# Top-k routing of 16 experts: places of the chosen tokens from a scan, indices sorted later, the gate applied at the addition

## The chip, the cores and the metric

One core of a Trainium2 chip runs the whole program in one launch. The metric is the device time of one execution in microseconds, the median of several runs. The core's engines are TensorE (PE in the profile; its weight loads are the row PEld), VectorE (DVE), ScalarE (ACT) and GpSimd (POOL). SyncE (SP) issues nearly all transfers from device memory.

## The reference

Two blocks one after the other on 256 tokens of width 1024, all float32. The change lies in the first block's expert layer:

```python
def _expert_choice_ffn(xn, router_w, w_gate, w_up, w_down):
    cap = EC_CAPACITY * T // N_EXPERTS                       # 2 * 256 / 16 = 32
    probs = softmax(einsum('btd,de->bte', xn, router_w))     # 256 tokens, 16 experts
    gate, idx = lax.top_k(swapaxes(probs, 1, 2), cap)        # each expert chooses 32 tokens
    xg = xn[bidx, idx]
    h = silu(einsum('becd,edf->becf', xg, w_gate)) * einsum('becd,edf->becf', xg, w_up)
    y = einsum('becf,efd->becd', h, w_down) * gate[..., None]
    return zeros_like(xn).at[bidx, idx].add(y)
```

Each expert's three matrices are 1024x2048, 1024x2048 and 2048x1024 in float32, 8 MB each, 24 MB an expert. The order of an expert's 32 tokens is free as long as gather, gate and scatter agree on it.

## The kernel before

The kernel is written engine by engine, each with its own list of instructions; semaphores (`S.name`, `wait_ge`) tie them together, so the order on an engine is the order in the code. `link(...)` on VectorE makes the next instruction wait until this one has ended.

The first mixer ends with the output product (`mix1_pe`, `mix1_dve`), which adds to the residual `hres` (128 tokens by two tiles by 1024). Then the routing: `route_transposes` and `route_rows` bring the normalised rows into channel order, 32 matmuls (line 836) give the logits, ScalarE and VectorE the softmax `probs` (lines 886 to 906: tokens in partitions, 16 experts wide). TensorE transposes it into `probT`: 16 partitions, 256 tokens wide.

On `probT` VectorE runs four rounds (lines 910 to 914), each finding the next 8 of the 32 largest (`max`), their indices (`max_index`) and overwriting them by -1 (`match_replace`). The indices as floats `topf` are spread into a block-diagonal `spread` of 16x512, which one matmul with ones broadcasts to all 128 partitions (line 847, `bank[4]`): in each partition the 512 token indices of 16 experts by 32 places. Two more matmuls (line 851) put the indices and the gates as columns into `bank[5]`. VectorE compares the broadcast with the token number of each partition (line 926): this gives `sel`, for each token tile a 0/1 matrix of tokens by (expert, place), first for the first pair of experts, then for the rest. `gather` (line 869) multiplies the normalised token rows with `sel`: 16 matmuls for a pair of experts, and `take_xg` (line 937) scales the result into `xg`, the input of the pair.

While VectorE searches, TensorE has nothing of use to do, and `keep_busy` (line 824) issues filler matmuls of 512 columns, whose result nobody reads: one in front of the transpose of the probabilities and six behind it.

The experts run in pairs (`expert_pair`). A piece of weights is 2 MB; an expert has 12 (4 gate, 4 up, 4 down), and 16 matmuls use a piece (lines 969 and 985). The pieces go through a ring of 8 slots; `slot_used` counts the pieces done, and SyncE (`experts_sync`, `load_slot`, line 1060) waits for it before it overwrites a slot. The very first piece lies in `early`, so nine pieces can be loaded before the first expert begins. Of each expert the chain is gate and up products, silu on ScalarE, product on VectorE (`hgu`, line 1035), transposes, down product, ScalarE's copy to `yo` times the gate (line 1018), and the scatter: a matmul with `selT` (line 997), which VectorE builds per expert by comparing `iota` with the column of indices `idx_now` (line 1032), and four additions to `hres` (line 1043). The first pair's code is written out (its index is the integer 0); the middle ones are a loop.

Behind the experts comes the second block, which neither the change nor its data touch.

## Time and profile before

| | |
|---|---|
| median of 3 runs | 1481.41 us (1478.77 to 1485.8) |
| the profiled execution | 1486.1 us, its span 1484.3 us, mean granted clock 0.874 |
| busy | PE 1103.4 (74%), PEld 630.8, VectorE 366.8 (25%), ScalarE 302.4, GpSimd 301.4 |
| the chain that ended last | DMA 56%, PE 37%, VectorE 5%, ScalarE 1% |
| memory | 475.88 MB read, 321 GB/s over the span |
| experts' weights | 191 transfers of 2048 KB into the ring, 35.7 to 36.0 us each from issue to landing |

In the rows below, times are us from the span's start. A row of the timeline gives start, duration, engine, line and operation, what it writes and reads, how many it merges, and in brackets the idle time before it with who ended it. In a row by stretch, each engine has its busy time and count; then come the clock granted to TensorE (1.00 is 2.4 GHz, 0.50 is 1.2 GHz), the busy share of the transfer engines and the bytes they moved. A float32 matmul appears as two passes.

### The profile page before, as it was taken

To read this page: it belongs to the slowest core of one execution; us is meant where nothing else is said; L and a number is where in the kernel's file an instruction comes from. 1 tells how busy PE (TensorE), PEld (TensorE's weight loads), DVE (VectorE), ACT (ScalarE), POOL (GpSimd) and SP (SyncE) were. 2 spreads that over 40 slices of the span, in tenths; PEclk is the share of its full clock that TensorE was granted. 3 is DMA by queue.
4 is the path that set the end of the run, shared out by engine and by line. 5 is a ranking of instruction groups with operands and counts; after the bars stand their busy time and mean duration, and the time that the engine had idled before them with its cause. 6 is when DMAs were issued, how large, how long until landed. Compare 5 with 4: busy or idle time off the path is not lost.

```text
span 1484.3 us, 19442 instructions
## 1 busy us (share of the span) xinstructions
PE 1103.4 (74%) x8303; PEld 630.8 (42%) x8303; DVE 366.8 (25%) x698; ACT 302.4 (20%) x435; POOL 301.4 (20%) x153
## 2 busy tenths in 40 slices
PE   6999986665766666656666665565668699899997
PEld 6998631211311211211211211121127688899996
DVE  5486510100100000001001000010026834653343
ACT  5753210000000000000000000000025335543431
POOL 5895000000000000000000000000015544376560
PEclk9999988968878878888887888888889799899999
DMA  9510989999999999999999999999997323466540
GB/s 283 171 33 23 425 329 429 426 428 428 428 428 429 429 427 429 429 427 429 429 427 430 428 427 429 429 427 428 428 393 180 98 91 109 158 200 196 170 143 29
DMA packets 94711, 478.04 MB, mean 322 GB/s; under 512 B 11035, under 2 KB 64154, under 8 KB 70074
## 3 DMA queue, kind: packets, MB, share of 16 engines
q1 hardware_dynamic: 94064, 476.28, 79.8%
q8 instruction: 48, 0.79, 0.2%
q10 hardware_dynamic: 585, 0.86, 0.2%
q14 instruction: 14, 0.11, 0.0%
HBM read 475.88 MB, written 1.25 MB: 321 GB/s over the span
## 4 chain that ended last, share of the span: by engine, by line
DMA 56%; PE 37%; DVE 5%; ACT 1%; issue 1%; SPq 0%; DVEq 0%; ACTq 0%
DMA ring<-in_expert_w_down 20%; DMA ring<-in_expert_w_gate 19%; PE bank L1238 19%; DMA ring<-in_expert_w_up 17%; PE bank L1975 4%; PE bank L969 4%; PE bank L985 1%; PE bank L409 1%; PE bank L426 1%; DVE work L1753 1%; DVE slot_r L1213 1%; PE bank L422 1%; PE bank L824 0%; PE bank L1389 0%; DVE work L1762 0%
## 5 line engine op out<-in xcount | busy, mean ns | idle before, releaser
L969 PE MATMUL bank<-ring,work 128*32 128x512 f32 x2032 | 315.8, 755 | 212.0 <-DMA ring<-in_expert_w_up 125.1
L969 PEld LDWEIGHTS bank<-ring,work 128*32 128x32 f32 x2032 | 61.9, 124 | 458.3 <-DMA ring<-in_expert_w_up 207.2
L1213 POOL TENSOR_TENSOR slot_r<-ring,slot_r 128x1024 fp32r<-128x1024 f32 (+1 forms) x60 | 217.9, 3646 | 136.1 <-ACT slot_r L1190 136.1
L985 PE MATMUL bank<-ring,work 128*32 128x512 f32 x1024 | 157.2, 748 | 91.4 <-DMA ring<-in_expert_w_down 88.0
L1221 POOL TENSOR_TENSOR slot_r<-ring,slot_r 128x512 fp32r<-128x512 f32 x16 | 21.5, 1363 | 975.8 <-ACT slot_r L1190 964.7
L1238 PE MATMUL bank<-slot_r 128*128 128x256 f32 (+1 forms) x1056 | 163.5, 296 | 10.3 <-DVE chan L2258 4.7
L1238 PEld LDWEIGHTS bank<-slot_r 128*128 128x128 f32 x1056 | 148.5, 202 | 14.7 <-DVE chan L2258 4.9
L1035 DVE TENSOR_TENSOR work<-work,bank 128x512 f32<-128x512 f32 x16 | 11.0, 687 | 511.5 <-PE bank L969 511.5
L1238 PE MATMUL bank<-work_r,slot_r 128*128 128x256 f32 x704 | 128.2, 283 | 1.2 <-DVE chan_r L1709 1.2
L1190 ACT ACTIVATE slot_r<-ring 128x2048 fp32r<-128x2048 f32 x63 | 118.3, 1903 | 1.8 <-DMA ring<-in_w_in 1.8
L1043 DVE TENSOR_TENSOR hres<-hres,bank 128x512 f32<-128x512 f32 x64 | 44.0, 687 | 299.3 <-PE bank L997 299.3
L985 PEld LDWEIGHTS bank<-ring,work 128*32 128x32 f32 x1024 | 31.7, 124 | 199.3 <-DMA ring<-in_expert_w_down 132.7
L1238 PEld LDWEIGHTS bank<-work_r,slot_r 128*128 128x128 f32 x704 | 110.3, 191 | 1.9 <-issue 1.5
L1238 PE MATMUL bank<-chan_r,slot_r 128*128 128x256 f32 x352 | 99.4, 283 | 0.0
L997 PE MATMUL bank<-chan,work 128*128 128x512 f32 x128 | 67.4, 665 | 13.2 <-ACT chan L1018 13.2
L1213 DVE TENSOR_TENSOR slot_r<-ring,slot_r 128x1024 fp32r<-128x1024 f32 x42 | 67.2, 1602 | 32.6 <-ACT slot_r L1190 32.5
L1018 ACT ACTIVATE chan<-bank,work 128x512 f32<-128x512 f32 x32 | 20.2, 683 | 266.6 <-PE bank L985 266.6
L1012 ACT ACTIVATE work<-bank 128x512 f32<-128x512 f32 x16 | 9.6, 597 | 313.9 <-PE bank L975 313.9
L1238 PEld LDWEIGHTS bank<-chan_r,slot_r 128*128 128x128 f32 x352 | 67.0, 190 | 0.4
L1010 ACT ACTIVATE work<-bank 128x512 f32<-128x512 f32 x16 | 9.6, 597 | 275.9 <-PE bank L969 275.9
L1975 PE MATMUL bank<-slot_r,work_r 128*128 128x512 f32 x264 | 63.1, 395 | 0.0
L1975 PEld LDWEIGHTS bank<-slot_r,work_r 128*128 128x128 f32 x264 | 48.9, 188 | 11.0
(388 smaller groups left out, 1025.8 us busy)
## 6 DMA issues: line engine op xcount, KB each, us to landing
ring<-in_expert_w_up SPq DMA_DIRECT2D x64, 2048.0 KB, 36.0
ring<-in_expert_w_down SPq DMA_DIRECT2D x64, 2048.0 KB, 35.8
ring<-in_expert_w_gate SPq DMA_DIRECT2D x63, 2048.0 KB, 35.7
ring<-in_w_in SPq DMA_DIRECT2D x23, 1024.0 KB, 8.1
ring<-in_w_ffn_gate SPq DMA_DIRECT2D x11, 1024.0 KB, 5.5
ring<-in_w_ffn_up SPq DMA_DIRECT2D x11, 1024.0 KB, 5.3
ring<-in_w_ffn_down SPq DMA_DIRECT2D x11, 1024.0 KB, 5.0
ring<-in_w_out SPq DMA_DIRECT2D x8, 1024.0 KB, 5.1
```

What stands on the lines that cost most here:

```text
L409: ins = pe.matmul(bank[2 * i][a, cs(h)], level_tile(i)[a, cs(h)], eye[a] if li == 0 else xm(i)[a, cs(h)], start=True, stop=True)
L422: ins = pe.matmul(wing(bank[2 * i + 1], 0)[a, cs(h)], xtm(i)[a, cs(h)], p1m(i)[a, cs(h)], start=True, stop=True)
L969: ins = pe.matmul(bank[b][32 * j:32 * j + 32, :], xg[:, 2 * s + kk, a * CAP:(a + 1) * CAP], w_[:, kk * FF + j * W5:kk * FF + (j + 1) * W5] ...
L985: ins = pe.matmul(bank[YB[dh]][32 * q:32 * q + 32, :], hT[:, q * P + 32 * s:q * P + 32 * s + 32], w_[:, q * D + dh * W5:q * D + (dh + 1) * ...
L997: pe.matmul(bank[(LAST_SB[t] if final else SB)[dh]][:, :], selT[:, t * P:(t + 1) * P], yo[:, dh * W5:(dh + 1) * W5], start=True, stop=True ...
L1018: act.activation(yo[:, dh * W5:(dh + 1) * W5], bank[YB[dh]][:, :], ACT.Copy, scale=gate_now)\
L1043: dve.tensor_tensor(part, part, bank[from_][:, :], ALU.add).then_inc(S.scat_added, 1)
L1190: act.activation(ring_r[s][:, UNIT:2 * UNIT], ring[:, s, 0:UNIT], ACT.Copy).then_inc(S.w_hi, 1)
L1213: eng.tensor_tensor(ring_r[s][:, at], ring[:, s, at], ring_r[s][:, at.start + UNIT:at.stop + UNIT].bitcast(F32), ALU.subtract).then_inc(S. ...
L1221: ins = eng.tensor_tensor(ring_r[s][:, at:at + q], ring[:, s, at:at + q], ring_r[s][:, at + UNIT:at + UNIT + q].bitcast(F32), ALU.subtract)
L1238: ins = pe.matmul(out_, x_, y_, start=first and i == 0, stop=last and i == 2, skip_group_check=apart)
L1975: ins = pe.matmul(bank[2 * t + half][:, :], a[:, f, tok], b[:, f, half * W5:(half + 1) * W5], start=(g == 0 and f == 0 and i == 0), stop=( ...
```

## The change

VectorE's four rounds lose the index search. What is left behind in `probT` is -1 where a token was chosen; a comparison makes `taken` (0/1, 16x256) of it. A scan (`tensor_tensor_scan`: state times 1 minus `taken`, from 33) counts down over the tokens, so that the first chosen token of an expert gets place 32 and the last one place 1; multiplied by `taken`, `places` is 0 for tokens not chosen. TensorE transposes `places` (two small transposes) to tokens in partitions, and `sel` comes from comparing it with 1 to 32. The broadcast matmul, the spread, the `memset` of two unused places and the two column matmuls go.

The indices, which only the scatter needs, come from `taken` times (token + 1): four rounds of `max` and `match_replace` sort them, in descending order, as the places are. Two rounds stand before `take_xg` of the first pair and two behind it. Their column is made by one matmul (`index_columns`), which TensorE issues after the gate product of expert 0. The gates are not sorted: ScalarE copies `yo` without a scale, and VectorE multiplies by the gate of the token when it adds to `hres`, with `probs` of the expert (`gate_now`, one buffer for each of a pair). The filler matmuls behind the transpose of the probabilities go from six to two.

```diff
@@ -775,21 +775,20 @@
         E = N_EXPERTS
         sems("route_out lmax_ready prob_exp prob_ready")
         sems("spread_ready sel_ready idx_cols_ready")
-        ROUTED = {"logits": 1, "probT": 2, "idx_bc": 3, "idx_col": 4}
+        ROUTED = {"logits": 1, "probT": 2, "places": 3, "idx_col": 4}
         rw = wab[:, :, :]
         probs = work(0)[:, 128:128 + TT * E].rearrange("p (t e) -> p t e", t=TT)
         lmax = work(0)[:, 160:162]
         lsum = work(0)[:, 162:164]
         probT = work(0)[0:E, 256:512]
-        tops = work(1)[0:E, 0:CAP]
-        topi = work(1)[0:E, 32:32 + CAP].bitcast(U32)
-        topf = work(1)[0:E, 64:64 + CAP]
-        spread = work(2)[0:E, :]
+        eight = work(1)[0:E, 0:8]
+        sorted_ = work(1)[0:E, 32:32 + CAP]
+        taken = work(2)[0:E, 0:T]
+        places = work(2)[0:E, T:2 * T]
         sel = work0[:, 3 * W5:3 * W5 + TT * (E + 2) * CAP].rearrange("p (t s) -> p t s", t=TT)
         idx4 = work(1)[:, 128:128 + E]
-        gate4 = work(1)[:, 160:160 + E]
         idx_now = work(1)[:, 192:193]
-        gate_now = work(1)[:, 193:194]
+        gate_now = (work(1)[:, 194:194 + TT], work(1)[:, 196:196 + TT])
         lexp = work(1)[:, 200:200 + TT * E].rearrange("p (t e) -> p t e", t=TT)
         xg = work(6).rearrange("p (k c) -> p k c", k=DK)
         selT = work(7)[:, 0:T]
@@ -842,13 +841,10 @@
                 ins = pe.transpose(bank[3][0:E, t * P:(t + 1) * P], probs[:, t, :], ident)
             ins.then_inc(S.route_out, 1)
             rel_pe(pe)
-            keep_busy(pe, 6)
+            keep_busy(pe, 2)
             pe.wait_ge(S.spread_ready, 1)
-            pe.matmul(bank[4][:, :], ones[0:E, :], spread, start=True, stop=True).then_inc(S.route_out, 1)
-            pe.wait_ge(S.spread_ready, 2)
-            for i in range(2):
-                src = cols4[i]
-                ins = pe.matmul(bank[5][:, i * E:(i + 1) * E], src, ident[0:E, 0:E], start=True, stop=True)
+            for t in range(TT):
+                ins = pe.transpose(bank[4][:, t * E:(t + 1) * E], places[:, t * P:(t + 1) * P], ident[0:E, 0:E])
             ins.then_inc(S.route_out, 1)
 
             pe.wait_ge(S.act_chain, 3)
@@ -856,7 +852,12 @@
             pe.wait_ge(S.normed_ready, NORMED["h1"] + TT)
             gather(pe, 0)
 
-        cols4 = (work(5)[0:E, 128:256], work(5)[0:E, 256:384])
+        cols4 = work(1)[0:E, 256:384]
+
+        def index_columns(pe):
+
+            pe.wait_ge(S.spread_ready, 2)
+            pe.matmul(bank[5][:, 0:E], cols4, ident[0:E, 0:E], start=True, stop=True).then_inc(S.route_out, 1)
 
         def pair_rows(t, k):
 
@@ -908,29 +909,37 @@
             link(dve.tensor_copy(probT, bank[3][0:E, 0:T]))
 
             for n in range(CAP // 8):
-                eight = tops[:, 8 * n:8 * n + 8]
                 link(dve.max(eight, probT))
-                dve.max_index(topi[:, 8 * n:8 * n + 8], eight, probT)
                 link(dve.match_replace(probT, eight, probT, -1.0))
-            link(dve.tensor_copy(topf, topi))
-            dve.tensor_tensor(spread.rearrange("p (a c) -> p a c", a=E), topf.unsqueeze(1).to_broadcast([E, E, CAP]),
-                              bc(ident[0:E, 0:E], [E, E, CAP]), ALU.mult).then_inc(S.spread_ready, 1)
-            dve.tensor_copy(cols4[0].rearrange("p (a c) -> p a c", a=4), topf.unsqueeze(1).to_broadcast([E, 4, CAP]))
-            dve.tensor_copy(cols4[1].rearrange("p (a c) -> p a c", a=4), tops.unsqueeze(1).to_broadcast([E, 4, CAP]))\
-                .then_inc(S.spread_ready, 1)
-            dve.memset(sel[:, :, E * CAP:], 0.0)
-            dve.wait_ge(S.route_out, ROUTED["idx_bc"])
-
-            for at in (slice(0, PAIR * CAP), slice(PAIR * CAP, E * CAP)):
+            link(dve.tensor_scalar(taken, probT, 0.0, None, ALU.is_lt))
+            link(dve.tensor_tensor_scan(places, ones[0:E, 0:1].to_broadcast([E, T]), taken, CAP + 1.0, ALU.mult, ALU.subtract))
+            dve.tensor_tensor(places, places, taken, ALU.mult).then_inc(S.spread_ready, 1)
+            dve.wait_ge(S.route_out, ROUTED["places"])
+
+            place = bank[4][:, 0:TT * E].rearrange("p (t e) -> p t e", t=TT)
+            for at in (slice(0, PAIR), slice(PAIR, E)):
                 for t in range(TT):
-                    ins = dve.tensor_scalar(sel[:, t, at], bank[4][:, at], const("tok")[:, t:t + 1], None, ALU.is_equal)
+                    n = at.stop - at.start
+                    ins = dve.tensor_tensor(sel[:, t, at.start * CAP:at.stop * CAP].rearrange("p (e c) -> p e c", c=CAP),
+                                            bc(place[:, t, at], [P, n, CAP]),
+                                            const("iota")[:, 1:CAP + 1].unsqueeze(1).to_broadcast([P, n, CAP]), ALU.is_equal)
                 ins.then_inc(S.sel_ready, 1)
+            link(dve.scalar_tensor_tensor(taken, const("iota")[0:E, :], 1.0, taken, ALU.add, ALU.mult))
+
+            def sort(rounds):
+                for n in rounds:
+                    link(dve.max(sorted_[:, 8 * n:8 * n + 8], taken))
+                    link(dve.match_replace(taken, sorted_[:, 8 * n:8 * n + 8], taken, 0.0))
+
+            sort((0, 1))
+            take_xg(dve, 1)
+            sort((2, 3))
+            dve.tensor_scalar(cols4.rearrange("p (a c) -> p a c", a=4), sorted_.unsqueeze(1).to_broadcast([E, 4, CAP]), -1.0, None,
+                              ALU.add).then_inc(S.spread_ready, 1)
+            link(dve.tensor_tensor(vec("norm_mix_2", 0, DK), vec("norm_mix_2", 0, DK), vec("norm_final_w", 0, DK), ALU.mult))
             dve.wait_ge(S.route_out, ROUTED["idx_col"])
-            dve.tensor_copy(idx4, bank[5][:, 0:E])
-            dve.tensor_copy(gate4, bank[5][:, E:2 * E]).then_inc(S.idx_cols_ready, 1)
-            link(dve.tensor_tensor(vec("norm_mix_2", 0, DK), vec("norm_mix_2", 0, DK), vec("norm_final_w", 0, DK), ALU.mult))
+            dve.tensor_copy(idx4, bank[5][:, 0:E]).then_inc(S.idx_cols_ready, 1)
             dve.wait_ge(S.idx_cols_ready, 1)
-            take_xg(dve, 1)
 
         def take_xg(dve, n):
             dve.wait_ge(S.gather_out, n)
@@ -970,6 +979,8 @@
                                                 w_[:, kk * FF + j * W5:kk * FF + (j + 1) * W5],
                                                 start=(s + kk == 0), stop=(s == 3 and kk == 1))
                         ins.then_inc(S.slot_used, 1)
+                    if isinstance(i, int) and i + a + part == 0:
+                        index_columns(pe)
                 pe.wait_ge(S.h_ready, PAIR * i + a + 1)
                 for q in range(4):
                     ins = pe.transpose(bank[TB][:, q * P:(q + 1) * P], hgu.rearrange("p (c q) -> p q c", q=4)[:, q], ident)
@@ -1013,9 +1024,8 @@
                 if last and a == PAIR - 1:
                     act.activation(warm, eps, ACT.Sqrt)
                 act.wait_ge(S.slot_used, SPE * (PAIR * i + a) + SPE)
-                act.wait_ge(S.selT_ready, PAIR * i + a + 1)
                 for dh in range(2):
-                    act.activation(yo[:, dh * W5:(dh + 1) * W5], bank[YB[dh]][:, :], ACT.Copy, scale=gate_now)\
+                    act.activation(yo[:, dh * W5:(dh + 1) * W5], bank[YB[dh]][:, :], ACT.Copy)\
                         .then_inc(S.y_ready, 1)
 
         def experts_dve(dve, link):
@@ -1027,7 +1037,7 @@
         def expert_pair_dve(dve, i, last=False):
             for a in range(PAIR):
                 dve.tensor_copy(idx_now, idx4[:, bass.ds(PAIR * i + a, 1)]).then_inc(S.gcols_now, 1)
-                dve.tensor_copy(gate_now, gate4[:, bass.ds(PAIR * i + a, 1)]).then_inc(S.gcols_now, 1)
+                dve.tensor_copy(gate_now[a].unsqueeze(2), probs[:, :, bass.ds(PAIR * i + a, 1)]).then_inc(S.gcols_now, 1)
                 dve.wait_ge(S.gcols_now, 2 * (PAIR * i + a) + 2)
                 dve.tensor_scalar(selT, const("iota"), idx_now, None, ALU.is_equal).then_inc(S.selT_ready, 1)
                 dve.wait_ge(S.silu_ready, PAIR * i + a + 1)
@@ -1040,7 +1050,8 @@
                         dve.wait_ge(S.scat_out, 4 * (PAIR * i + a) + 2 * t + dh + 1)
                         part = hres[:, t, dh * W5:(dh + 1) * W5]
                         from_ = (LAST_SB[t] if last and a == PAIR - 1 else SB)[dh]
-                        dve.tensor_tensor(part, part, bank[from_][:, :], ALU.add).then_inc(S.scat_added, 1)
+                        dve.scalar_tensor_tensor(part, bank[from_][:, :], gate_now[a][:, t:t + 1], part, ALU.mult, ALU.add)\
+                            .then_inc(S.scat_added, 1)
 
         wg3 = io["expert_w_gate"]
         wu3 = io["expert_w_up"]
```

## Rows read from the trace of the kernel before

**Rows 1.** The chain that ended last, 140 to 260 us: start us, us, what
```profile
178.27 7.09 PE bank L824 x12
185.36 1.05 PE bank L847 x2
...
187.03 5.83 PE bank L869 x32
...
193.73 16.50 PE bank L969 x128
...
210.24 28.09 DMA ring<-in_expert_w_gate
```

**Rows 2.** Busy time by stretch: last three columns granted clock, DMA share, GB/s
```profile
157.00:190.00 33.00, 31.31 (x140) 21.17 (x139) 14.78 (x47) 7.84 (x15) 0.00 (x0) 0.87 1.01 429
...
193.00:198.00 5.00, 4.27 (x21) 0.99 (x24) 1.22 (x4) 0.00 (x0) 0.00 (x0) 0.50 0.01 2
...
300.00:1080.00 780.00, 492.96 (x2896) 130.53 (x2892) 55.65 (x110) 38.97 (x58) 0.00 (x0) 0.82 1.01 428
```

**Rows 3.** Timeline of the SyncE queue, 195 to 216 us: the restart
```profile
199.94 3.76 SPq L1060 DMA_DIRECT2D ring<-in_expert_w_down  x3
```

**Rows 4.** Timeline of VectorE, 150 to 280 us: start us, us, line, op
```profile
176.95 0.42 DVE L912 MAX8 work<-work 16x8 f32<-16x256 f32 x1
...
182.37 0.17 DVE L915 CAST work<-work 16x32 f32<-16x32 uint32 x1
182.57 0.68 DVE L916 TENSOR_TENSOR work<-work,cst 16x512 f32<-16x512 f32 x1
...
186.45 1.66 DVE L926 TENSOR_SCALAR work<-bank,cst 128x64 f32<-128x64 f32 x4 [2.79 <-PE bank L847]
```

**Rows 5.** Timeline of VectorE in the second block's top-k, 1120 to 1186 us
```profile
1159.72 0.43 DVE L1761 MAX8 work<-work 128x8 f32<-128x256 f32 x1
...
1160.70 0.43 DVE L1761 MAX8 work<-work 128x8 f32<-128x256 f32 x1
...
1167.59 0.29 DVE L1763 TENSOR_SCALAR work<-work 128x256 f32<-128x256 f32 x1
```

**Rows 6.** VectorE by line and shape: count, busy us, mean ns, idle before
```profile
L1043 DVE TENSOR_TENSOR hres<-hres,bank 128x512 f32<-128x512 f32 x64 | 44.0, 687 | 299.3 <-PE bank L997 299.3
...
L732 DVE TENSOR_TENSOR chan<-ring,bank 128x256 f32<-128x256 f32 x8 | 2.8, 414 | 1.6 <-PE bank L467 1.6
...
L757 DVE SCALAR_TENSOR_TENSOR early<-bank,vecT,early 128x512 f32<-128x512 f32 x2 | 1.4, 747 | 2.1 <-PE bank L494 2.1
...
L926 DVE TENSOR_SCALAR work<-bank,cst 128x448 f32<-128x448 f32 x2 | 1.3, 676 | 0.0
```

**Rows 7.** The scans of line 1773: ns min/median/max, first and last start
```profile
L1773 DVE TENSOR_TENSOR_SCAN work<-cst,work x2: 692/2859/5026, 1144.4 to 1145.1; 128x256 f32<-128x256 f32 x2
```

**Rows 8.** Timeline of GpSimd, 1138 to 1186 us
```profile
1145.02 4.54 POOL L1213 TENSOR_TENSOR slot_r<-ring,slot_r 128x2048 fp32r<-128x2048 f32 x1 [5.49 <-ACT slot_r L1190]
```

**Rows 9.** GpSimd's busy time from 150 to 1100 us
```profile
150.00:1100.00 950.00, 0.00 (x0) 0.83 1.00 424
```

**Rows 10.** Busy time by stretch around routing, for the granted clock
```profile
175.00:181.00 6.00, 5.13 (x8) 1.45 (x9) 4.62 (x18) 3.05 (x6) 0.00 (x0) 0.50 1.02 434
181.00:182.00 1.00, 1.00 (x3) 0.45 (x2) 0.95 (x5) 0.00 (x0) 0.00 (x0) 0.63 1.04 442
188.70:193.00 4.30, 4.15 (x20) 3.96 (x19) 0.02 (x1) 0.00 (x0) 0.00 (x0) 0.50 0.68 282
261.00:265.20 4.20, 4.20 (x40) 4.13 (x43) 0.01 (x1) 0.60 (x1) 0.00 (x0) 1.00 0.99 421
```

**Rows 11.** Timeline of TensorE, 150 to 280 us: first pieces, second gather
```profile
193.73 3.64 PE L969 MATMUL bank<-early,work 128*32 128x512 f32 x16 [0.88 <-DVE work L937]
...
225.41 1.92 PE L969 MATMUL bank<-ring,work 128*32 128x512 f32 x16
...
261.27 3.88 PE L869 MATMUL bank<-work,tokm 128*128 128x64 f32 x32
```

## The prediction

> **What bounds the kernel now.** I read the chain that ended last first, then the memory traffic by stretch, then the SyncE queue, then the two engines around the routing, TensorE's granted clock last.
>
> The chain [rows 1] runs through TensorE and VectorE until 210.24 us, then it turns to weight transfers (the first of 28 us) with a few matmuls between them. That second part is the 16 experts. In it the memory runs at 428 GB/s from 300 to 1080 us, as it does before 190 us while the ring is filled for the first time [rows 2]. So the experts are bound by weight traffic, and no engine's time inside them counts.
>
> The traffic has one hole at the routing: 429 GB/s up to 190 us, 2 GB/s from 193 to 198 us [rows 2]. All eight ring slots and `early` are then full, and SyncE can't issue the next piece before the first ring piece has been used; it issues again at 199.94 us [rows 3]. Everything behind that moment, the 183 remaining pieces and the second block, follows from it. An edit to the routing is therefore worth what it moves that restart, and it moves it one for one: the last preloaded piece is in between 190 and 193 us, before TensorE asks for it, so the preload doesn't catch a shift of a few us.
>
> What sets the restart, from the chain [rows 1]: filler matmuls of `keep_busy` 178.27 to 185.36, the broadcast of the indices until 186.4, the first comparison on VectorE (starts at 186.45 [rows 4]), gather 187.03 to 192.86, scaling of `xg`, experts from 193.73. Two pieces later the restart. Note who was late at 185.36: VectorE had `spread` ready at 182.57 + 0.68 = 183.25 us [rows 4], so the **filler** was the last to come, by 2.1 us.
>
> **The change, part by part.** I start from the first `max` at 176.95 us [rows 4], which nothing in front of it moves.
> - The four rounds took until the cast at 182.37, 1.36 us each [rows 4]. Without the index search a round is what the second block's top-k shows: 1160.70 - 1159.72 = 0.98 us [rows 5], on 128 partitions in place of 16. Four rounds: 3.92, end 180.87.
> - `taken`, a comparison of 256 elements: the like row is 0.29 us [rows 5], plus 0.03 for the chained wait: 181.19.
> - The scan over 256 elements: the trace has two, of 0.69 and 5.03 us [rows 7]. I take 0.69 and 0.03 of wait, 181.91; why the other doesn't apply is told with the rivals.
> - places times taken, 256 elements: 0.41 us [rows 6]: 182.32.
> - PE's two small transposes instead of the broadcast and the two column matmuls. No row has their shape (16 rows in, 16 columns wide). The nearest from below is nothing but the hand-over, some 0.1 us; from above the broadcast's 1.05 us in the chain [rows 1]. They stream 16 columns and not 512, so I take a value near the lower half, 0.5, estimated between the two: 182.82, and 0.04 to VectorE. TensorE is free by then: the six fillers took 7.09 us [rows 1], the first part of it at the half clock (0.50 until 181, a mean of 0.63 from 181 to 182, so full from about 181.75 [rows 10]). That is 3.5 / 2 + 3.6 = 5.35 us of full clock, 0.9 each; two of them at the half clock take 3.6 and end near 181.8. From 6 to 2 removes the late arrival named above; had the 6 stayed, the gain of VectorE's part would be nil. The first comparison starts at 182.86 where it was 186.45: **3.6 us earlier**.
> - The comparisons are now `tensor_tensor` from PSUM, 64 and 448 elements as before, one PSUM operand as before: no change taken, bounds -0.1 and +0.3.
> - While the gather runs, VectorE does the two long comparisons (0.68 each [rows 6]), the index product (at most 0.75, the price of the form 512 wide [rows 6]) and two rounds of sorting (1.96): 4.1 us. The gather that hides it took 5.8 us [rows 1]; if it ran at full clock, 3.88 [rows 11], the cover is used up and costs 0.2.
> - The second half of the sort, the columns and the vector product (about 2.3 us) stand behind `take_xg` and before the expert's own VectorE work. `index_columns` waits for them on TensorE, with the rest of expert 0 queued behind it; but it stands behind 64 matmuls that take until about 203, and VectorE is done near 193. It costs its own matmul, some 0.4 us, at a moment when the traffic is running again: nothing. Without that cover it would be up to 2.3 us.
> - In the loop: `gate_now` copies two columns instead of one, the additions become `scalar_tensor_tensor`. 512 elements cost 0.75 at most as against 0.69 [rows 6], 64 times 0.06 = 4 us of VectorE time in 900 us in which it waits. Memory hides it; only the last, about 0.06, stands at the end, against which ScalarE's copy loses its scale and its wait on `selT`. Nothing.
> - The `memset`, two column copies, `gate4`: off the chain once the index columns are. Nothing more.
>
> The clock. The gather began at full clock, ran at 0.50 from 188.7 on [rows 10], and took 5.8 us; the same gather later, wholly at full clock, took 3.88 [rows 10, 11]. The first expert piece took 3.64 at 0.50 against 1.92 later [rows 2, 11]. After the change TensorE does less before the gather: two fillers, half a microsecond of rest, two transposes, a short rest. The clock rose before 182 us [rows 10] on work that the change leaves in place, and fell at 188.7 in the gather, whose matmuls are short beside their weight loads. I take both stretches, gather and first two pieces, as long as now. Bounds: all at full clock is -1.9 for the gather and 2 x 1.92 = 3.8 instead of 199.9 - 193.7 = 6.2 for the pieces, -2.3; all at half is 2 x 3.88 = 7.8, +1.9, and 7.3 to 7.7, +1.4.
>
> Sum: -3.6. The profiled execution would go from 1484.3 us of span (1486.1 in all) to 1480.7. Its 1486.1 lie 4.7 above the median of the runs shown, 1481.41; the -3.6 applied to that median give, **1477.8 us**.
>
> **The rivals.**
> 1. The clock holds. If it stays at full through the shorter gather (it needs to hold until about 187.3, and fell at 188.7 here) and is up again for the first pieces, -3.6 - 1.9 - 2.3 + 0.2 = -7.6: 1473.8. For it: the gather starts 3.6 earlier, nearer to the fillers. Against: two thirds of the filler is gone, and the pieces of expert 0 began at 0.50 in the trace [rows 2]. Half of it (only the gather) gives 1475.9. Chance of the whole 0.12, the part lies in the forecast's range.
> 2. The clock falls with the filler, before the gather: transposes 0.2 longer, +1.9, +1.4: -0.1, 1481.3. For: the filler stood there directly before the gather, and it goes. Against: it was the fall at 188.7, not the filler's end, that ended the full clock, and that is 3 us behind the filler. Chance 0.2.
> 3. The scan costs its dear price and the kernel is slower. The two scans of the trace began at 1144.4 and 1145.1; beside the second one GpSimd had an addition from 1145.02 for 4.54 us [rows 8], and the scan ended with it. At 5.03 the chain is 4.34 longer: -3.6 + 4.3 = +0.7, 1482.1. It decides from a scan of 4.3 us on. Against: GpSimd has nothing to do from 150 to 1100 us [rows 9], and nothing in the change gives it anything. Chance 0.04. The Trainium skill has this as a rule (SBUF — State Buffer, Who interferes with whom): a VectorE instruction with two SBUF inputs and a GpSimd one that reads SBUF share a read port under an exclusive lock, and the later one is blocked to the end of the first. By that rule, the trace agrees (5.03 beside the 4.54, 0.69 without), the second scan's price is the neighbour's, and with GpSimd idle the 0.69 holds.
> 4. The change does nothing to the end: the restart is tied to something else than the slot, such as a data transfer. Then 1481.4. Against: 2 GB/s while TensorE works. Chance 0.04.
>
> **How the numbers follow.** Forecast 0.60, at 1477.8, with its own range of 1475 to 1480. The rivals hold 0.40, as above. Range: 1473.8 at the lower end and 1482.1 at the upper; the runs shown of before spread by +4.4 and -2.6, so a median of a few has an uncertainty of about 1.5 by itself: 1472.5 to 1483. 0.5% is 7.4 us, about what a measurement of this kernel can tell from no change. Only rival 1 comes up to it: faster 0.12. Nothing above comes near it on the other side; what stays is a median disturbed or a wait not seen: slower 0.05; same 0.83.
>
> **What would show it.** Four rounds in 3.9 us and a scan of 0.7 on the VectorE timeline; the end of the filler before VectorE's signal; the first comparison 5.9 us behind the first `max` (before: 9.5); gather and first piece at the clock assumed; SyncE's next issue at about 196.3; the memory hole shorter by the same, and 428 GB/s from there on. The prediction is wrong if the gather is not the next thing that waits (the sort holding up `xg`), if the scan is longer than 0.7, or if the clock is the other one of its two levels in the gather and the first pieces.

## The result

| | median, us | runs | range |
|---|---|---|---|
| kernel before | 1485.20 | 9 | 1478.50 to 1493.94 |
| changed kernel | 1475.81 | 9 | 1472.85 to 1484.05 |

The ratio is 0.995, with a 95% interval of 0.9928 to 0.9972: faster by 0.3 to 0.7%. The forecast was 1477.8 us in a range of 1472.5 to 1483.0, so the time is in the range and of the forecast sign. The difference between the two medians is 9.4 us, however (by the ratio's interval 4 to 11 us), and the forecast sum was 3.6. The experiments are about that gap. The profiled execution of the changed kernel has a span of 1471.1 us, 13.2 less than that of before; the forecast for it was 1480.7.

The chain that ended last in the changed kernel, 140 to 260 us (start, us, what). It answers to [rows 1].

```profile
181.65 0.42 DVE work L916
...
182.12 0.29 PE bank L847 x2
...
182.91 5.22 PE bank L870 x32
...
188.96 8.57 PE bank L978 x64
197.53 0.32 PE bank L860 x2
197.85 7.05 PE bank L978 x64
...
204.92 27.54 DMA ring<-in_expert_w_gate
```

The filler is gone from the chain. VectorE's last product hands over to two transposes of 0.29 us, and the gather starts at 182.91 us where it started at 187.03. `index_columns` shows as 0.32 us between the two products of expert 0.

The changed kernel's VectorE timeline, 172 to 232 us, answers to [rows 4]; below it the SyncE queue, as in [rows 3].

```profile
176.79 0.42 DVE L912 MAX8 work<-work 16x8 f32<-16x256 f32 x1
...
177.75 0.42 DVE L912 MAX8 work<-work 16x8 f32<-16x256 f32 x1
...
180.62 0.28 DVE L914 TENSOR_SCALAR work<-work 16x256 f32<-16x256 f32 x1
180.94 0.68 DVE L915 TENSOR_TENSOR_SCAN work<-cst,work 16x256 f32<-16x256 f32 x1
181.65 0.41 DVE L916 TENSOR_TENSOR work<-work 16x256 f32<-16x256 f32 x1
182.45 1.42 DVE L923 TENSOR_TENSOR work<-bank,cst 128x64 f32<-128x64 f32 x4 [0.39 <-PE bank L847]
...
188.22 0.69 DVE L946 TENSOR_TENSOR work<-bank,cols 128x512 f32<-128x512 f32 x1 [2.12 <-PE bank L870]
...
197.96 0.17 DVE L941 COPY work<-bank 128x16 f32<-128x16 f32 x1 [6.93 <-PE bank L860]
```

```profile
194.17 3.76 SPq L1071 DMA_DIRECT2D ring<-in_expert_w_down  x3
```

A round takes 177.75 - 176.79 = 0.96 us. The scan takes 0.68 us. `take_xg` at 188.22 waited 2.12 us for the gather, so the half sort ahead of it was hidden; the copy of the index column at 197.96 waited 6.93 us for TensorE, so the other half was hidden too. SyncE resumes at 194.17 us (before 199.94).

TensorE's granted clock in the changed kernel, by stretch (last three columns: clock, DMA share, GB/s):

```profile
182.00:185.00 3.00, 2.39 (x20) 2.32 (x21) 2.54 (x9) 0.00 (x0) 0.00 (x0) 1.00 0.99 423
186.00:188.50 2.50, 2.11 (x10) 1.92 (x10) 0.39 (x2) 0.00 (x0) 0.00 (x0) 0.50 1.07 443
188.90:191.90 3.00, 2.94 (x16) 0.79 (x20) 1.99 (x9) 0.00 (x0) 0.00 (x0) 0.50 0.88 371
192.00:197.00 5.00, 5.00 (x52) 1.32 (x44) 0.00 (x0) 1.28 (x1) 0.00 (x0) 1.00 0.69 194
```

Full clock for the transposes and the start of the gather, half from 186 us on (the stretch from 185 to 186 us shows a mean of 0.60, so it fell some 2.3 us into the gather), full again from 192: the first piece of expert 0 ran at half clock as before, the second no longer.

In the loop, by line and shape (count, total, mean ns):

```profile
L1053 DVE SCALAR_TENSOR_TENSOR hres<-bank,work,hres 128x512 f32<-128x512 f32 x64 | 48.0, 751 | 296.5 <-PE bank L1008 293.3
...
L1028 ACT ACTIVATE chan<-bank 128x512 f32<-128x512 f32 x32 | 17.4, 594 | 267.5 <-PE bank L996 267.5
```

The additions cost 751 ns (687 in [rows 6]), ScalarE's copy without its scale 594 (683 with it, in the kernel before).

### The profile page after: what moved, and what is told of

It reads as the page before. It is cut to its first block, busy times and chain, and to the rows that moved or that the text cites. A ratio compares the mean times of both kernels' runs of the same rounds, so it can differ in the third digit from the quotient of the medians.

```text
span 1471.1 us, 19410 instructions
## 1 busy us (share of the span) xinstructions
PE 1098.6 (75%) x8293; PEld 625.8 (43%) x8293; DVE 368.3 (25%) x701; ACT 299.6 (20%) x435; POOL 301.3 (20%) x153
## 4 chain that ended last, share of the span: by engine, by line
DMA 57%; PE 38%; DVE 4%; ACT 1%; issue 1%; SPq 0%; DVEq 0%; ACTq 0%
PE bank L1249 20%; DMA ring<-in_expert_w_down 20%; DMA ring<-in_expert_w_gate 19%; DMA ring<-in_expert_w_up 17%; PE bank L1986 4%; PE bank L978 4%; PE bank L996 1%; PE bank L409 1%; PE bank L426 1%; DVE slot_r L1224 1%; PE bank L422 1%; PE bank L1400 0%; PE bank L1418 0%; DVE work L1784 0%; PE bank L870 0%
## 5 line engine op out<-in xcount | busy, mean ns | idle before, releaser
L1053 DVE SCALAR_TENSOR_TENSOR hres<-bank,work,hres 128x512 f32<-128x512 f32 x64 | 48.0, 751 | 296.5 <-PE bank L1008 293.3
L1028 ACT ACTIVATE chan<-bank 128x512 f32<-128x512 f32 x32 | 17.4, 594 | 267.5 <-PE bank L996 267.5
```

The costliest lines, as they stand in the source:

```text
L1028: act.activation(yo[:, dh * W5:(dh + 1) * W5], bank[YB[dh]][:, :], ACT.Copy)\
L1053: dve.scalar_tensor_tensor(part, bank[from_][:, :], gate_now[a][:, t:t + 1], part, ALU.mult, ALU.add)\
```

## The experiments

All milestones below are read in the same way from each kernel's profile: the start of the first comparison, the gather's duration, the start of the first expert matmul, and SyncE's first issue behind it (the restart). All but the duration are us from the first `max`, so that what lies ahead drops out. That is needed: the first `max` itself lies anywhere from 175.50 to 179.49 us in the thirteen profiles.

| kernel | comparison | gather takes | experts | restart |
|---|---|---|---|---|
| before | 9.50 | 5.82 | 16.78 | 22.99 |
| before, 2 fillers | 7.51 | 7.06 | 16.03 | 22.54 |
| before, quarters | 9.30 | 5.97 | 16.74 | 22.76 |
| changed | 5.66 | 5.21 | 12.17 | 17.38 |
| changed, again | 5.67 | 5.56 | 12.54 | 19.04 |
| changed, halves | 5.66 | 6.06 | 13.03 | 18.98 |
| changed, quarters | 5.66 | 5.93 | 12.90 | 18.99 |
| changed, 3 fillers | 5.82 | 3.95 | 11.08 | 16.46 |
| changed, 4 fillers | 6.50 | 3.95 | 11.77 | 15.47 |
| changed, 6 fillers | 8.29 | 3.95 | 13.55 | 17.25 |

### The changed kernel again

> The changed kernel as it is, beside the kernel before on the same chip. Theory A (the gain is what the restart of the weight traffic moves): restart at 194 to 196 us against 199 to 200 us, and the time lower by 4 to 6 us. Theory B (besides, the profile's 13 us hold a chance part: in the second block VectorE's mask comparison took 4.61 us in the kernel before and 0.23 us in the changed one, because a GpSimd operation held the shared port): then the time differs by 5 to 10 us from one execution to another in both kernels, and this profile may show the comparison at 4.6 us again with a span 4 us longer.

Measured: 1475.60 us, ratio 0.9948 (0.9924 to 0.9972): 9.5 us below the median of the kernel before, where theory A has 4 to 6. The restart is at 197.37 us, later than the 194 to 196 expected, but its first `max` also came 1.5 us later than in the other profile; counted from there the restart is 3.95 us earlier than before, against 5.61 in the first profile. The difference between the two profiles of one kernel shows in the clock: the second half of the logits' matmuls ahead of the first `max` took 3.15 us in place of 1.94; and in the first profile it was full again 3.1 us after the experts' start, in this one only after some 5.7. The span is 1475.8 us. Part of it was lost at the experts' end, where the last product and the scatter ran at half clock:

```profile
1098.51 3.69 PE bank L996 x16
...
1102.96 6.14 PE bank L1008 x8
```

In the first profile of the changed kernel they took 1.97 and 3.69.

The mask comparison, described in the next section, was short here too (0.23 and 0.29 us for its two widths), as in every profile of the changed kernel. So expectation B's "may show the comparison at 4.6 us again" didn't come. The 27 times of the kernel before beside these runs fall into two groups, 9 from 1477.6 to 1480.7 and 18 from 1484.3 to 1488.0, with nothing between. Of the changed kernel's ten, nine lie from 1472.3 to 1477.7 and one at 1483.1; of the nine behind the result above, two more stand apart, at 1480.2 and 1484.1.

This gives an estimate of what the routing is worth, apart from the groups: the lower group of before has a mean of 1478.7 us, the nine of the changed kernel 1475.1, a difference of 3.6. The rest of the difference between the two means (1483.7 and 1475.9) is that the kernel before falls more often into the upper group, whose mean is 1486.2.

### Where the kernels meet GpSimd in the second block

The mask comparison (`dve.tensor_scalar(addm[t], sc, TAKEN, NEG, ALU.not_equal, ALU.mult)`) ends the choice of the 64 keys. In the kernel before, its source line (ns min/median/max, starts), and GpSimd's timeline:

```profile
L1763 DVE TENSOR_SCALAR work<-work x2: 293/2452/4610, 1167.6 to 1176.9; 128x256 f32<-128x256 f32 x1, 128x128 f32<-128x128 f32 x1
```

```profile
1172.22 9.16 POOL L1213 TENSOR_TENSOR slot_r<-ring,slot_r 128x2048 fp32r<-128x2048 f32 x2 [15.61 <-ACT slot_r L1190]
```

The same two views in the changed kernel:

```profile
L1774 DVE TENSOR_SCALAR work<-work x2: 230/262/293, 1161.2 to 1170.4; 128x256 f32<-128x256 f32 x1, 128x128 f32<-128x128 f32 x1
```

```profile
1165.77 4.60 POOL L1224 TENSOR_TENSOR slot_r<-ring,slot_r 128x2048 fp32r<-128x2048 f32 x1 [15.49 <-ACT slot_r L1201]
1171.13 9.14 POOL L1224 TENSOR_TENSOR slot_r<-ring,slot_r 128x2048 fp32r<-128x2048 f32 x2 [0.76 <-ACT slot_r L1201]
```

In the kernel before, GpSimd's two subtractions of 4.6 us follow each other without a gap; the comparison of 0.23 us comes due at 1176.85, when the second has just begun, and ends with it after 4.61 us. In the changed kernel GpSimd had to wait 0.76 us for ScalarE between the two, and the comparison at 1170.40 went through that gap. The dear scan (5.03 us) was met in both profiles alike, so it has no part in the difference. What made the gap stands on TensorE (timelines of the kernel before and of the changed one), the 96 passes behind an idle stretch of 11 us:

```profile
1159.27 12.70 PE L1238 MATMUL bank<-slot_r 128*128 128x256 f32 x96
```

```profile
1152.93 14.00 PE L1249 MATMUL bank<-slot_r 128*128 128x256 f32 x96
```

They were 1.3 us slower, since the clock rose later in them (in the kernel before it had a mean of 0.66 from 1160 to 1162 us and 1.00 after, so it rose some 2 us into the stretch; in the changed kernel it was 0.50 to 1158 us, 5 us into it). ScalarE's next high part waits for a product behind them, and GpSimd for ScalarE. A slower TensorE made this execution faster.

The other profiles fit. In the two of the kernel before that have GpSimd's operations whole (with six and with two fillers) the clock rose 2.1 and 2.2 us into these passes, GpSimd had no gap, and the comparison took 4.61 and 4.59 us. In the six of the changed kernel that have them whole it rose 4.0 to 5.2 us into them, GpSimd had a gap of 0.28 to 0.81 us, and the comparison took 0.23.

The comparison cost more than its own 4.4 us, since TensorE waits behind it. The chain that ended last, in the kernel before and below it in the changed one:

```profile
1183.31 1.11 PE bank L1372 x2
...
1186.99 2.00 PE bank L1380 x4
1188.99 7.34 PE bank L1238 x48
```

```profile
1174.36 0.57 PE bank L1383 x2
...
1176.24 1.06 PE bank L1391 x4
1177.30 5.95 PE bank L1249 x48
```

In the kernel before TensorE stood idle for 3.92 us in front of 1183.31, waiting for VectorE, and then had a granted clock of 0.50 until 1192 us: from there to the end of the 48 passes it took 13.0 us. In the changed kernel it didn't stand idle, had 1.00, and took 8.9. The bill of the second block is then 3.92 + 4.13, less the 1.30 that the 96 passes were quicker, and 0.5 in front of these: 7.2 us, of the 7.3 by which the second block was longer in the kernel before.

### GpSimd's operations in halves and quarters

```diff
-                split_low(pool, SECOND_FIRST + n, False)
+                split_low_pieces(pool, SECOND_FIRST + n, 4)   # 2 in the version with halves
...
+            for i in range(pieces):
+                at = i * width
+                ins = eng.tensor_tensor(ring_r[s][:, at:at + width], ring[:, s, at:at + width],
+                                        ring_r[s][:, at + UNIT:at + UNIT + width].bitcast(F32), ALU.subtract)
```

> The changed kernel; in the second block each of GpSimd's subtractions that split a weight unit (8 places in the code, 128x2048 or 128x1024) is done as two of half the width. Theory B (an operation of GpSimd holds the port to its end): the second scan, which took 5.03 us beside a GpSimd operation of 4.54, takes 2.7 to 3.0, and the mask comparison never more than 2.6; the time 2 to 4 us below the changed kernel. Rival (VectorE's wait there is covered by other work, or GpSimd's added start costs take it back): scan shorter, time within 1 us.

Measured: 1475.41 us, ratio 0.9938 (0.9915 to 0.9960). The dear scan fell from 5.03 to 2.89 us. Against the 1475.60 of the version with whole operations, though, the median didn't move (2 to 4 us lower was expected); its highest time of six is 1476.8 (1483.1 there). Half a result: the mechanism as expected, the gain not visible.

> The kernel before; in the second block each of GpSimd's subtractions that split a weight unit is done in four pieces of a quarter of the width. Theory B (the kernel before falls into two groups of times, 1477.6 to 1480.7 and 1484.2 to 1488.0 us, because VectorE's mask comparison sometimes meets a GpSimd operation that holds the shared port for 4.6 us): the comparison never takes more than 1.5 us, the scan 1.3 to 1.8 instead of 5.03, the upper group is gone, and the median is 1474 to 1478 us, 7 to 10 below the kernel before. Rival (the two groups come from TensorE's clock alone): both groups stay, each at most 3 us lower.

> The changed kernel with the same quartered GpSimd operations. Against the kernel before with quarters only the routing differs, so what is left is the restart of the weight traffic: theory A 4 to 6 us below that kernel, about 1470 to 1473 us. If the difference is under 2 us, most of what the change was measured to give came from meeting the GpSimd operation less often and not from the routing.

Measured:

| | median, us | times |
|---|---|---|
| before, quarters | 1475.90 | 1474.68, 1475.85, 1475.96, 1477.82 |
| changed, quarters | 1472.24 | 1469.94, 1471.95, 1472.53, 1473.83 |

Their ratios to the kernel before are 0.9945 (0.9925 to 0.9965) and 0.9915 (0.9893 to 0.9938). The scan and the mask comparison in the kernel before with quarters:

```profile
L1784 DVE TENSOR_TENSOR_SCAN work<-cst,work x2: 691/1234/1778, 1143.5 to 1144.2; 128x256 f32<-128x256 f32 x2
```

```profile
L1774 DVE TENSOR_SCALAR work<-work x2: 293/383/473, 1164.6 to 1173.9; 128x256 f32<-128x256 f32 x1, 128x128 f32<-128x128 f32 x1
```

The scan's worst is 1.78 us, the comparison's 0.47, and the upper group of times is gone: none of the four is above 1477.8, while the kernel before's 19 executions beside these have both groups again (5 up to 1481.3, 14 from 1484.1). Theory B holds: the upper group goes with the length of GpSimd's operations. And with the wait for GpSimd small in both kernels (1.78 and 0.5 us at most), what the changed routing gives is 1475.90 - 1472.24 = **3.7 us**, where the prediction's sum had 3.6 and theory A 4 to 6. All four times of the one lie below all four of the other, so the sign is sure; the size is not, with four executions each an uncertainty of some 2.5 us either way (an estimate from their spread), and that it comes so near to 3.6 is in part luck. The two profiles can't confirm it: counted from the first `max` the restart is 3.8 us earlier, but the spans differ by 2.7, with the experts ending 5.2 us earlier and the second block 2.5 us longer.

Of the 9.4 us between the medians the rest, some 5.7, is by subtraction the second block's, which the change doesn't touch: 18 of 27 executions of the kernel before fall into the upper group and 1 of 10 of the changed one.

### The filler

```diff
-            keep_busy(pe, 2)
+            keep_busy(pe, 6)      # and 3, and 4; the kernel before: 6 to 2
```

> The kernel before with two filler matmuls in place of six, the index search kept. Theory A: the broadcast starts when VectorE has spread ready, 183.3 us in place of 185.36; first comparison near 184.4, the restart 2 us earlier, the time 2 us below the kernel before: about a third of the change's gain. Rival (the clock falls without the filler): the gather takes 6.5 to 7.8 us in place of 5.8 and the restart is at most 0.5 us earlier.

Measured: 1480.68 us, ratio 0.9983 (0.9959 to 1.0008). Its TensorE timeline:

```profile
183.37 1.12 PE L847 MATMUL bank<-work,cst 16*128 16x512 f32 x2 [1.44 <-DVE work L916]
...
185.11 7.06 PE L869 MATMUL bank<-work,tokm 128*128 128x64 f32 x32 [0.26 <-issue]
```

The broadcast indeed followed `spread` (183.37 us), the first comparison came 2.0 us earlier. But the clock fell near 185.1 us, as the gather began, and it took 7.06 us, 1.24 longer: of 2.0 us only 0.45 reached the restart (22.99 to 22.54). By the profile the rival is right, and taking late filler away gave almost nothing by itself. The times can't settle it: the median is 4.5 us below the 1485.13 of the kernel before, but the interval holds 1, and the ten times stand in both groups.

> The changed kernel with six filler matmuls in place of two. Theory A (the filler's end was the late arrival, VectorE's shorter work alone brings nothing): places are ready at about 182.1 us, the fillers end at about 185.2, first comparison 185.5 to 185.6, gather from 186.0 (changed kernel: 182.91), the restart 3 us later than in the changed kernel, the time 3 us above it. Rival (the filler holds the clock): the gather runs longer at full clock and takes 4.0 to 4.6 us in place of 5.2, and the first pieces are quicker, so that the restart is less than 1.5 us later.

Measured: 1481.01 us, ratio 0.9975 (0.9953 to 0.9997). Its TensorE timeline:

```profile
180.47 6.79 PE L823 MATMUL bank<-cst 128*128 128x512 f32 x12
...
187.97 3.95 PE L870 MATMUL bank<-work,tokm 128*128 128x64 f32 x32 [0.50 <-issue]
192.78 1.92 PE L978 MATMUL bank<-early,work 128*32 128x512 f32 x16 [0.85 <-DVE work L946]
```

The comparison is 2.6 us later than with two fillers, as theory A has it. Gather and first piece ran at full clock, 3.95 and 1.92 us, and the restart is level with the best profile with two (17.25 against 17.38 to 19.04): the rival again, in this profile. The times say otherwise. Their median is 5.4 us above that of the changed kernel beside them (1475.60), they spread from 1474.3 to 1487.5, and the profiled execution is the fastest of the ten. Whether the slower ones lose in the routing or in the second block isn't shown.

> The changed kernel with three filler matmuls in place of two. The profile with six showed the gather at full clock in 3.95 us (5.2 to 6.1 with two), which paid back the 2.6 us that the fillers ended late. If one filler more suffices to hold the clock through the gather: fillers end 6.6 to 6.9 us behind the first max, first comparison at most 1 us later, gather 4 to 4.5 us, restart 1 to 3 us earlier than in the changed kernel. If it doesn't: gather 5 to 6 us and the restart 0.5 us later.

Measured: 1472.75 us, ratio 0.9941 (0.9918 to 0.9964); gather 3.95 us, restart 16.46, 0.9 to 2.6 us earlier than with two. Three of the ten times lie apart, from 1479.6 to 1483.0.

> The changed kernel with four filler matmuls. Fillers end 7.0 to 7.6 us behind the first max, the first comparison 1.4 to 2 us later than with two. Clock held: gather 3.9 to 4.3 us and quicker first pieces, restart 1 to 2 us earlier than with two. Clock not held: restart 1.5 us later than with two, the time 1.5 us above it.

Measured: 1477.42 us, ratio 0.9954 (0.9934 to 0.9975), but spread from 1470.9 to 1483.5. In the profile, again of the fastest execution, gather and first piece are at full clock and the restart is the earliest of this series, 15.47; the first comparison is 0.8 us later than with two, where 1.4 to 2 was expected:

```profile
177.11 5.00 PE L823 MATMUL bank<-cst 128*128 128x512 f32 x8
...
182.82 3.95 PE L870 MATMUL bank<-work,tokm 128*128 128x64 f32 x32 [0.49 <-issue]
187.63 1.92 PE L978 MATMUL bank<-early,work 128*32 128x512 f32 x16 [0.85 <-DVE work L946]
```

### Filler and quarters together

> The changed kernel with three fillers and the quartered GpSimd operations together. Both act at different places: 1469 to 1472 us, no time above 1475, 0 to 2 us below the changed kernel with quarters alone (1472.2). If the third filler only chose luckier moments in the second block, the two are equal within 0.5 us.

> The same with four fillers. With four, the profile had gather and first pieces all at full clock, restart 15.5 us behind the first max against 17.4 to 19.0 with two; if that holds in most executions 1468 to 1471 us, otherwise 0.5 to 1.5 us above the version with three.

Measured: 1470.16 us (1468.44 to 1470.82), ratio 0.9904 (0.9884 to 0.9924), and 1469.60 us (1466.96 to 1471.17), ratio 0.9897 (0.9876 to 0.9919). With quarters alone it was 1472.24. Restart at 16.88 and 15.46 us behind the first `max`, where the quarters alone have 18.99. Both are below the kernel before and the changed one. Against quarters alone they are 2.1 and 2.6 us lower, as the restart has it, but the intervals of the ratios overlap; between three and four fillers these six executions each can't decide.

### A GpSimd operation beside the routing's scan

```diff
+            dve.wait_ge(S.pool_chain, 12)      # VectorE, in front of the product of norm_mix_2
...
+            pool.wait_ge(S.dve_chain, 53)      # the fourth max
+            for _ in range(2):
+                link(pool.tensor_tensor(chan[:, 4:8, :], hres[:, 0].rearrange("p (k t) -> p k t", k=4),
+                                        hres[:, 1].rearrange("p (k t) -> p k t", k=4), ALU.add))
```

> The changed kernel with two GpSimd additions of 128x1024 (two SBUF inputs, results read by nobody) that start when VectorE has found the fourth eight; they run beside the last replacement, the comparison, the scan and the product. The third rival of the prediction (the scan pays for a GpSimd operation beside it): the stretch from the fourth max to the first comparison, 2.8 us in the changed kernel, grows by 2 to 5 us, and one of VectorE's instructions in it shows 2 to 4.6 us in place of its 0.3 to 0.7. If the port matters only for wide work on all partitions (here VectorE uses 16): nothing grows by more than 0.3 us.

Measured, VectorE's and GpSimd's timelines of that kernel:

```profile
182.31 0.42 DVE L912 MAX8 work<-work 16x8 f32<-16x256 f32 x1
...
183.27 2.02 DVE L914 TENSOR_SCALAR work<-work 16x256 f32<-16x256 f32 x1
185.33 2.78 DVE L915 TENSOR_TENSOR_SCAN work<-cst,work 16x256 f32<-16x256 f32 x1
188.14 0.41 DVE L916 TENSOR_TENSOR work<-work 16x256 f32<-16x256 f32 x1
189.03 1.41 DVE L923 TENSOR_TENSOR work<-bank,cst 128x64 f32<-128x64 f32 x4 [0.48 <-PE bank L847]
```

```profile
182.81 4.75 POOL L2092 TENSOR_TENSOR chan<-hres 128x1024 f32<-128x1024 f32 x2 [40.02 <-DVE work L912]
```

The comparison grew from 0.28 to 2.02 us and the scan from 0.68 to 2.78; each waited for one of GpSimd's two additions: the scan, begun at 185.33, ended at 188.11, 0.55 us behind the second (182.81 + 4.75 = 187.56). From the fourth `max` to the first comparison it is 189.03 - 182.31 = 6.7 us in place of 2.8, and the restart is 23.1 us behind the first `max`, where the changed kernel has 17.4 to 19.0. One execution, 1481.2 us. The third rival's price is real, 16 partitions don't save from it, and GpSimd's idleness is what kept it away.

## Why the prediction was right, and where it was not

**The bound and the restart.** Right. SyncE resumed 5.8 us earlier, and the experts' last addition ended 5.9 us earlier (1102.8 against 1108.7). One for one, as said, holds to the start of the experts' last product: 5.8 us earlier in this profile, and 2.9 earlier with a restart 2.6 earlier in the second one. It doesn't hold past it: in the second profile the last product and the scatter ran at half clock, and the last addition ended at 1109.9, later than before.

**VectorE's part.** Forecast 5.91 us from the first `max` to the first comparison, measured 5.66 or 5.67 in the four profiles of the changed kernel with two fillers and GpSimd idle. By terms: four rounds 3.83 (forecast 3.92), `taken` 0.32 (0.32), scan 0.71 (0.72), product 0.42 (0.41), hand-over and transposes 0.38 (0.54). The value between two far ends, the transposes, was the largest miss, 0.16 us. That nothing moves the first `max`, from which all this counts, holds for the edit but not for single executions (175.50 to 179.49 us).

**"From 6 to 2 removes the late arrival."** The mechanism was seen, its worth misjudged. The prediction charged the filler's lateness and credited it nothing; "had the 6 stayed, the gain of VectorE's part would be nil" was wrong. With six in the changed kernel the first comparison was 1.2 us earlier than before and the restart 5.7, in the profile. With two fillers in the kernel before, 2.0 us of lateness went and 1.2 came back in the gather, 0.3 in the first pieces. In the changed kernel two are one or two too few by the profiles; the times show it for neither number alone (1472.75 with three, 1477.42 with four, 1475.60 with two).

**The clock.** "I take both stretches as long as now": near enough. The gather took 5.2 to 6.1 us with two fillers, 5.8 before, and the restart was 3.95 to 5.6 us earlier. The bounds (all full, all half) hold every profile to 0.1 us (the first two pieces took 3.7 us at their shortest, 3.8 was the bound). Rival 2's gather of 7.8 us was nearly met (7.06) by the kernel before with two fillers. Rival 1, worth -7.6 us, wants the clock held; with four fillers it is, in the profile: 22.99 - 15.47 = 7.5 us.

**Hidden work.** Right: both halves of the sort, the index column, the loop's additions. 64 times 0.06 us was 64 times 0.064.

**"Everything behind that moment follows from it".** This step failed. The second block's length isn't fixed: in the two profiles, from the experts' last addition to the end of the span, it took 1484.3 - 1108.7 = 375.6 and 1471.1 - 1102.8 = 368.3 us, 7.3 us of the 13.2, nearly all of it the mask comparison's wait for GpSimd and TensorE's idle time and half clock behind it. The prediction had the row that says why, 5.03 us for a scan [rows 7, 8], and used it only to ask whether it could happen in the routing, not whether its likes in the second block come and go between executions and kernels. The three times shown of before (1478.8, 1481.4, 1485.8) stood on both sides of a gap that was read as noise.

**The numbers.** 1477.8 was worked from a median of three, 1481.4, which belongs to the lower group or stands just above it. Against the 1485.2 of nine the same sum would have given 1481.6, 5.8 too high. That the forecast came within 2 us of 1475.81 is luck: a base that was 3.8 us too low made up for most of a gain in the second block that wasn't foreseen. Rival 3, the slower side, was out for the reason given. The chance of "faster by over 0.5%", 0.12, was too low given what the runs showed: the measured ratio lies on that line, and in the kernel before two executions of three fall into the upper group.

**Open.** Why the changed kernel meets the port so much less often is only argued: the profiles show TensorE's clock rising later in the 96 passes, and the two profiles with the long comparison (the kernel before with six and with two fillers) had an early rise (12.70 and 12.74 us for the passes, against 14.00 and 13.79 in two of the changed kernel's). That this is a lasting consequence of the new timing and not of the few profiles isn't shown, and one profile speaks against it: in the changed kernel with quarters the clock rose early too, 2.0 us into the passes, which took 12.66. Nor is it shown what the upper group's executions of the changed kernel lose; no profile of them was taken, and none of the kernel before in its lower group.

## What to carry to other kernels

Before a difference of medians is put down to an edit, look whether the times of either kernel fall into groups, and remove the cause of the groups from both: here 9.4 us became 3.7. Filler matmuls that end late are not lost time when the product behind them runs at full clock for it; count both, and try the number. Where VectorE and GpSimd share a stretch, the length of GpSimd's single operations is a price on VectorE's chain; cutting them into quarters took 9.2 us off the median of the kernel before (1485.07 to 1475.90).

## What the runs showed of the hardware

- A VectorE comparison of 0.23 us took 4.6, and a scan of 0.69 took 5.03, beside one GpSimd operation of 4.5 to 4.6 us; with that operation in two pieces the scan took 2.89, in four 1.78. They end 0.1 to 0.6 us behind the operation that is running (the profile counts the wait as their duration), so the length of one piece counts. The Trainium skill (SBUF — State Buffer, Who interferes with whom) says that whoever of VectorE and GpSimd issues first holds their shared pair of ports for its whole instruction and the other is blocked. The trace agrees; it shows the same for VectorE work on 16 partitions (0.68 became 2.78).
- The clock's rise moves the end of the program in both directions. The last product and the scatter of the experts took 1.97 + 3.69 us at full clock and 3.69 + 6.14 at half, in two profiles of one kernel; and a later rise in the second block went with a comparison that was 4.4 us shorter.
- A wait of VectorE can cost TensorE its clock: idle for 3.92 us behind the long comparison, TensorE fell to 0.50 and took 13.0 us for what took 8.9 at 1.00.
- In the changed kernel with two fillers and GpSimd idle the clock fell 1.2 to 2.3 us into the gather (at its start in the kernel before with two fillers); with three or more it fell not before the gather's end: 3.95 us in all five profiles with three, four or six. The number alone doesn't decide: in the kernel before, with six fillers and the broadcast behind them, it fell 1.7 us into the gather, which took 5.82.
